# Expert results stored to DRAM and fetched by token, instead of scattered by matmul

## The chip, the cores and the metric

The kernel runs on one core of one Trainium2 chip. The metric is the device time of one execution in microseconds (us), as the median of three runs. A core has TensorE (PE, with PEld its weight loads), VectorE (DVE), ScalarE (ACT), GpSimd (POOL) and SyncE (SP), each with its own queue of instructions; they wait for one another by semaphores. DMA engines move data between DRAM and the core's memories.

## The reference

Four transformer layers over 256 tokens of width 1024, all in f32: two of a first kind, two of a second. The last block of the last layer is a mixture of eight experts, and only this block and what surrounds it are touched:

```python
logits = (xt @ w_router).astype(jnp.float32)
top_vals, top_idx = lax.top_k(logits, TOP_K)          # TOP_K = 2 of 8 experts
probs = jax.nn.softmax(top_vals, axis=-1)
combine = jnp.sum(jax.nn.one_hot(top_idx, N_EXPERTS) * probs[..., None], axis=1)
# for each expert:
acc = acc + c[:, None] * ((silu(xt @ wg) * (xt @ wu)) @ wd)     # wg, wu: 1024 x 2816
# and then
x = layer_norm(DN_ALPHA * x + acc, ln2_g, ln2_b)
```

## The kernel before

Every f32 product is made of three matmuls: an operand is split into a high part (ScalarE's copy, `e_hi`, `ring_hi`) and the rest (VectorE's subtraction, `e_lo`, `ring_lo`); high x high, low x high and high x low are summed in PSUM (`product`, L707 to L709).

An expert handles up to 128 tokens, its slots; were any expert chosen by more than 128 tokens, a second pass over all experts (numbers 8 to 15) would follow under `If(over > 0)`. With the inputs here it is skipped. An expert's weights, 34.6 MB, are cut in 48 units of 704 KB. SyncE loads them into eight buffers (`e_raw`, `expert`, L576) as TensorE frees them (`w_used`); ScalarE makes the high part (L2174), VectorE the low part in place (L3043), TensorE multiplies. Units 0 to 7 and 16 to 23 are the gate's, 8 to 15 and 24 to 31 the up projection's, for one half of the hidden width each; 32 to 47 are the down projection's. Between them VectorE does the gating product (L3049), TensorE transposes it (L1629), ScalarE and VectorE split it (L2183, L3056). Each engine has its order written out by unit number in a loop body (`expert_pe`, `expert_act`, `expert_dve`); expert 0 is unrolled and experts 1 to 7 are a hardware loop (`Fori`).

The tokens of an expert: one-hot tables from ranks (`slots`, L2989) give, by a tiny matmul (`token_of_slot`, L1600), the token of each slot; GpSimd fetches those rows of X from DRAM (`expert_pool`, L3286) and TensorE turns them (`gather`, L1594).

The results: an expert's output stands in the two PSUM banks `Sp` by slot. During the next expert ScalarE evicts its high part (`result`, L2167), VectorE makes its low part (`result_low`, L3028) and one-hot tables slot to token (`slots_to_tokens`, L3032), TensorE multiplies table and result for each half of the tokens (`scatter`, L1606, L1607, behind units 3 and 7), and VectorE adds the sum, times the token's weight for that expert, to the accumulator `ACC` (`add_back`, L2998). After the loop each engine tests for overflow (L1685 on TensorE) and loads the number of experts run; the last expert's result goes the same way in halves (L1694, L1695, L3114), then the norm and the output follow. `ACC` is cleared on VectorE behind the mixer of the last layer (`route_tables`, L2917), and ALPHA x X is added to it behind the last expert (L3105).

Of the kernel before, what the change touches and what calls it, by code (L numbers as in the profile page):

```python
# [134 lines left out]
def build(nc, at, n_const, const_d, w, out_d):  # L135
# [45 lines left out]
    FLAG = sb("FLAG", [P, 2], I32)  # L181
    TOKEN = sb("TOKEN", [P, NTB, 2], F32R)
    ROWS = sb("ROWS", [P, 1], U32)
    rows_d = nc.dram_tensor("rows_of_x", (S, D), F32, kind="Internal").ap()

# [146 lines left out]

    hEh = parts_at("hEh", arena_base, 0, [P, FT2, P])
# [8 lines left out]
    HBe = ar(2 * FT2 * S + HALF, HALF).rearrange("p (j q) -> p j q", j=JT)  # L342
    YBh = parts_at("YBh", arena_base, om + 2560, [P, D])
# [16 lines left out]
    ANY = ar(om + 4608 + 296, NTB * NE).rearrange("p (t e) -> p t e", t=NTB)  # L360
    ROUTE = G[:, 0:NTB, 0:2 * NE].rearrange("p t (w e) -> p t w e", w=2)
# [62 lines left out]
    m_yh, m_y = sig("e_y_high_part"), sig("e_y_taken")  # L424
    m_sc, m_acc = [sig("e_scattered0"), sig("e_scattered1")], sig("tables_cleared_then_e_added")
# [89 lines left out]
    def _(sp):  # L515
# [63 lines left out]
        with sp.Fori(0, NE) as i:  # L579
            expert(i, i)  # L580
        sp.wait_ge(m_flag.sem, 1)
        over = sp.value_load(FLAG[0:1, 0:1], min_val=0, max_val=1)
        with sp.If(over > 0):
            with sp.Fori(NE, 2 * NE) as i:
                expert(i, i - NE)

# [77 lines left out]
    def _(pe):  # L664
# [938 lines left out]
        def scatter(tb):  # L1603
            for h in range(2):
                cs = slice(h * 512, (h + 1) * 512)
                pe.matmul(Sp[:, h, :], PmT[:, tb, :], YBh[:, cs], start=True, stop=False)  # L1606
                last = pe.matmul(Sp[:, h, :], PmT[:, tb, :], YBl[:, cs], start=False, stop=True)  # L1607
            last.then_inc(m_sc[tb].sem, 1)

# [6 lines left out]
        def expert_pe(i, first=False):  # L1616
# [31 lines left out]
            for j in range(4 * KT):  # L1648
# [7 lines left out]
                if j == 3 and not first:  # L1656
                    pe.wait_ge(m_y.sem, i)
                    scatter(0)
                if j == KT - 1 and not first:
                    pe.wait_ge(m_acc.sem, 2 * i + 2)  # L1660
                    scatter(1)
                if first and j == KT:
                    token_of_slot(1)
                if j == KT + 4:
                    if not first:
                        pe.wait_ge(m_acc.sem, 2 * i + 3)
                    pe.wait_ge(m_p.sem, i + 2)
                    token_of_slot(0)
                if j == 2 * KT + 1:
                    hidden_e(0)  # L1670
            pe.wait_ge(m_t.sem, i + 1)
# [5 lines left out]
            gather(i + 1)  # L1677
# [3 lines left out]
        with pe.Fori(1, NE) as i:  # L1681
            expert_pe(i)
        pe.wait_ge(m_flag.sem, 1)
        over = pe.value_load(FLAG[0:1, 0:1], min_val=0, max_val=1)
        with pe.If(over > 0):  # L1685
            with pe.Fori(NE, 2 * NE) as i:
                expert_pe(i)
        n_all = pe.value_load(FLAG[0:1, 1:2], min_val=NE, max_val=2 * NE)
        pe.wait_ge(m_gd.sem, n_all + 1)
# [9 lines left out]
    def _(act):  # L1699
# [464 lines left out]
        def result(n):  # L2164

            act.wait_ge(w_used.sem, n * UNITS_E + U0)
            nc.scalar.activation(YBh[:, :], Sp[:, :, :].rearrange("p b n -> p (b n)"), ACT.Copy).then_inc(m_yh.sem, 1)  # L2167

        def expert_act(i, first=False):
# [15 lines left out]
            for j in range(UNITS_E):  # L2185
                if j == ACT_AHEAD and not first:
                    act.wait_ge(m_p.sem, i + 1)
# [16 lines left out]
                if j == 5 * KT + 2 + ACT_AHEAD:  # L2204
# [4 lines left out]
        with act.Fori(1, NE) as i:  # L2209
            expert_act(i)  # L2210
        act.wait_ge(m_flag.sem, 1)
        over = act.value_load(FLAG[0:1, 0:1], min_val=0, max_val=1)
        with act.If(over > 0):
            with act.Fori(NE, 2 * NE) as i:
                expert_act(i)
        n_all = act.value_load(FLAG[0:1, 1:2], min_val=NE, max_val=2 * NE)
        act.wait_ge(w_used.sem, n_all * UNITS_E + U0)
# [17 lines left out]
    def _(dve):  # L2235
# [455 lines left out]
        for l in range(DEPTH):  # L2691
# [224 lines left out]
            def route_tables():  # L2916
                do(v.memset(ACC, 0.0), m_acc)  # L2917
                do(v.memset(RK, 1e6), m_acc)
                do(v.memset(CW, 0.0), m_acc)
# [75 lines left out]
        def add_back(i, tb):  # L2995
            dve.wait_ge(m_sc[tb].sem, i)
            dve.wait_ge(m_acc.sem, i * 2 + (tb + 1))
# [330 lines left out]
```

## Time and profile before

| | us |
|---|---|
| median of three runs (lowest, highest) | 2000.38 (1999.57, 2001.59) |
| span of the profiled execution, its first to its last instruction | 1997.8 |
| TensorE busy | 1971.7 |
| VectorE busy | 1586.5 |
| ScalarE busy | 1226.4 |
| GpSimd busy | 98.7 |

The page gives no other time of the profiled execution than its span. Engines work side by side, so busy times don't add up; matmuls are pipelined, so their durations overlap and the distance of two starts is what one costs. An idle time is named by what ended it. Times of instructions are from the span's start. The experts' weights are the last 790 us of it.

### The profile page before, as it was taken

What the parts mean: (1) busy time and instruction counts of PE and PEld (TensorE: products, weight loads), DVE (VectorE), ACT (ScalarE), POOL (GpSimd) and SP (SyncE); (2) the same over time, 40 slices, a digit from 0 to 9 for tenths busy, and PEclk for the clock granted to TensorE, in tenths of its full rate; (3) what the DMA queues carried; (4) which work ended last, traced back from release to release, by engine and by line L of the source; (5) the groups of instructions that cost most, each with busy time, mean ns of one, the idle gap of its engine ahead of it and who ended that gap; (6) DMA issues with size and microseconds to landing.
All of it is one profiled execution on the core that took longest, in us unless ns stands there. A gap on an engine that the chain in (4) does not pass through costs nothing.

```text
span 1997.8 us, 30577 instructions
## 1 busy us (share of the span) xinstructions
PE 1971.7 (99%) x11807; PEld 1679.3 (84%) x11807; DVE 1586.5 (79%) x1630; ACT 1226.4 (61%) x1323; POOL 98.7 (5%) x163
## 2 busy tenths in 40 slices
PE   8999999999999999999999999999999999999997
PEld 6888888888888898888889888888888888888886
DVE  7787745868774579776658878999999899999997
ACT  6665534566553457455536537777777777777775
POOL 0400000040000000000000000000000000000000
PEclk9999999999999999999999999999999999999999
DMA  8326555632655555075545209999999999999995
GB/s 302 120 90 212 190 190 179 217 117 95 206 190 190 184 201 168 3 236 190 190 169 196 101 19 388 362 362 366 365 358 368 360 366 365 364 364 363 366 361 199
DMA packets 154089, 481.08 MB, mean 241 GB/s; under 512 B 14608, under 2 KB 41728, under 8 KB 153856
## 3 DMA queue, kind: packets, MB, share of 16 engines
q1 hardware_dynamic: 150064, 465.46, 64.7%
q0 software_dynamic: 3920, 14.16, 2.0%
q8 instruction: 74, 1.21, 0.2%
q14 instruction: 31, 0.25, 0.0%
HBM read 477.48 MB, written 2.10 MB: 240 GB/s over the span
## 4 chain that ended last, share of the span: by engine, by line
PE 91%; DVE 6%; ACT 1%; DMA 1%; issue 1%; POOL 1%; SPq 0%; DVEq 0%; POOLq 0%; ACTq 0%
PE G L707 16%; PE G L709 16%; PE G L708 16%; PE Sp L707 5%; PE Sp L709 5%; PE Sp L708 5%; PE G L1212 3%; PE G L734 3%; PE G L1511 3%; PE G L1213 2%; PE G L694 1%; DVE ring_lo L2251 1%; PE G L1512 1%; PE G L689 1%; PE G L690 1%; PE Sp L1212 1%
## 5 line engine op out<-in xcount | busy, mean ns | idle before, releaser
L2174 ACT ACTIVATE e_hi<-e_raw 128x1408 fp32r<-128x1408 f32 x384 | 523.8, 1381 | 156.4 <-DMA e_raw<-in_moe_w_gate 64.2
L3043 DVE TENSOR_TENSOR e_lo<-e_raw,e_hi 128x1408 fp32r<-128x1408 f32 x384 | 601.9, 1620 | 20.1 <-ACT e_hi L2174 17.6
L2251 DVE TENSOR_TENSOR ring_lo<-ring,ring_hi 128x2048 fp32r<-128x2048 f32 (+2 forms) x171 | 383.5, 2254 | 183.2 <-ACT ring_hi L1714 181.8
L1714 ACT ACTIVATE ring_hi<-ring 128x2048 fp32r<-128x2048 f32 (+1 forms) x179 | 335.5, 1883 | 227.5 <-PE G L709 109.7
L707 PE MATMUL G<-e_hi,xgTh 128*128 128x512 f32 (+1 forms) x768 | 289.2, 377 | 0.1
L709 PE MATMUL G<-e_hi,xgTl 128*128 128x512 f32 (+1 forms) x768 | 288.5, 376 | 0.0
L708 PE MATMUL G<-e_lo,xgTh 128*128 128x512 f32 (+1 forms) x768 | 287.1, 374 | 0.0
L708 PEld LDWEIGHTS G<-e_lo,xgTh 128*128 128x128 f32 x768 | 144.2, 188 | 23.9
L709 PEld LDWEIGHTS G<-e_hi,xgTl 128*128 128x128 f32 x768 | 144.0, 188 | 23.0
L707 PEld LDWEIGHTS G<-e_hi,xgTh 128*128 128x128 f32 x768 | 144.3, 188 | 22.7 <-DVE e_lo L3043 0.4
L707 PE MATMUL G<-ring_hi,xT 128*128 128x512 f32 (+2 forms) x360 | 140.4, 390 | 0.0
L707 PE MATMUL Sp<-e_hi,hEh 128*128 128x512 f32 x352 | 138.4, 393 | 0.0
L709 PE MATMUL G<-ring_hi,xT 128*128 128x512 f32 (+2 forms) x360 | 137.5, 382 | 0.0
L709 PE MATMUL Sp<-e_hi,hEl 128*128 128x512 f32 x352 | 137.4, 390 | 0.0
L708 PE MATMUL G<-ring_lo,xT 128*128 128x512 f32 (+2 forms) x360 | 137.4, 382 | 0.0
L708 PE MATMUL Sp<-e_lo,hEh 128*128 128x512 f32 x352 | 137.2, 390 | 0.0
L1212 PE MATMUL G<-xT,ring_hi 128*128 128x512 f32 x288 | 100.8, 394 | 0.0
L707 PE MATMUL G<-ring_hi,hTh 128*128 128x512 f32 x256 | 100.0, 391 | 0.0
L709 PE MATMUL G<-ring_hi,hTl 128*128 128x512 f32 x256 | 99.7, 389 | 0.0
L708 PE MATMUL G<-ring_lo,hTh 128*128 128x512 f32 x256 | 99.6, 389 | 0.0
L1213 PE MATMUL G<-xT,ring_lo 128*128 128x256 f32 x288 | 79.9, 277 | 0.0
L707 PEld LDWEIGHTS G<-ring_hi,xT 128*128 128x128 f32 x360 | 67.6, 188 | 14.5 <-issue 1.8
(480 smaller groups left out, 3589.9 us busy)
## 6 DMA issues: line engine op xcount, KB each, us to landing
e_raw<-in_moe_w_gate SPq DMA_DIRECT2D x128, 704.0 KB, 6.0
e_raw<-in_moe_w_up SPq DMA_DIRECT2D x128, 704.0 KB, 6.0
e_raw<-in_moe_w_down SPq DMA_DIRECT2D x128, 704.0 KB, 5.9
ring<-in_w_in SPq DMA_DIRECT2D x48, 1024.0 KB, 5.1
ring<-in_w_mlp_up SPq DMA_DIRECT2D x32, 1024.0 KB, 5.2
ring<-in_w_mlp_down SPq DMA_DIRECT2D x32, 1024.0 KB, 4.8
ring<-in_w_out SPq DMA_DIRECT2D x16, 1024.0 KB, 4.8
ring<-in_ffn_w_gate SPq DMA_DIRECT2D x22, 512.0 KB, 3.6
```

Of the source, the lines that this page charges most:

```text
L689: pe.matmul(out, ah, bh, start=start, stop=False, **kw)
L707: pe.matmul(out, ah, bh, start=start, stop=False, **kw)
L708: pe.matmul(out, ah, bl, start=False, stop=False, **kw)
L709: return pe.matmul(out, al, bh, start=False, stop=stop, **kw)
L734: last = pe.transpose(dst, src, ident[0:k, 0:k])
L1212: pe.matmul(out.rearrange("p (w s) -> p w s", w=2), bh[:, k, ms_], xT[:, :, kk, :], start=kk == 0, stop=False, skip_group_check=True)
L1213: last = pe.matmul(out[:, 0:S], bl[:, k, ms_], xTh[:, kk, :], start=False, stop=kk == KT - 1, skip_group_check=True)
L1511: pe.matmul(out.rearrange("p (w s) -> p w s", w=2), bh[:, k, ms_], xT[:, :, kk, :], start=kk == 0, stop=False, skip_group_check=True)
L1714: nc.scalar.activation(ring_hi[:, n % H, 0:m], ring[:, n % R, 0:m], ACT.Copy).then_inc(w_hi.sem, 1)
L2174: nc.scalar.activation(e_hi[:, u, :], e_raw[:, u, :], ACT.Copy).then_inc(w_hi.sem, 1)
L2251: v.tensor_tensor(ring_lo[:, n % R, cs], ring[:, n % R, cs], ring_hi[:, n % H, cs].bitcast(F32), ALU.subtract).then_inc(w_lo.sem, 1)
L3043: v.tensor_tensor(e_lo[:, u, :], e_raw[:, u, :], e_hi[:, u, :].bitcast(F32), ALU.subtract).then_inc(w_lo.sem, 1)
```

## The change

The result of an expert is evicted whole by ScalarE, as f32, into `YB`, and GpSimd stores these 128 rows (512 KB) to a DRAM buffer `y_d` of 16 x 128 rows, one block for each expert run (16 for the second pass). VectorE computes for each token the two rows of `y_d` that hold its results (`rows_of_y`, behind unit 40 of expert 0), and sets `ACC` to ALPHA x X (`scaled_x`, behind units 24 and 28 of expert 0). Both look-ups, for both halves of the tokens, are four fetches by index, which GpSimd issues when the results of experts 0 to 6 are stored; VectorE adds them, times the token's weights, behind units 24, 28, 32 and 36 of the last expert (`y_rows_added`). Therefore the last expert is written out apart, behind the loop (experts 1 to 6) and the test for overflow, on every engine but GpSimd's, with the number of the last run in a register. Its own result still goes by matmul. A token whose row is not yet written (its second expert is the last, or its slot is beyond 128) points to a row of zeros: nine blocks of `y_d`, 7 to 15, are stored as zeros by GpSimd from a cleared buffer of its own, `YZERO`, after the first norm of the third layer. `scatter`, `add_back`, `result_low`, the clearing of `ACC`, the last expert's gather and one `token_of_slot` of expert 0 are gone; `slots_to_tokens` is left for the last result only. Two declarations of semaphores are left out below.

```diff
@@ -178,10 +178,12 @@
-    FLAG = sb("FLAG", [P, 2], I32)
+    FLAG = sb("FLAG", [P, 3], I32)
...
+    YROWS = sb("YROWS", [P, 2 * NTB], U32)
...
+    y_d = nc.dram_tensor("rows_of_y", (2 * NE * P, D), F32, kind="Internal").ap()
@@ -330,6 +332,7 @@
+    YZERO = ar(2 * FT2 * S + 2048, D)
@@ -340,6 +343,7 @@
+    YB = ar(om + 2560, D)
@@ -358,6 +362,11 @@
+    RANKED = ar(om + 4608 + 320, 2 * NTB * NE).rearrange("p (w t e) -> p w t e", w=2, t=NTB)
+    YROW = ar(om + 4608 + 352, 2 * NTB)
+    YLIM = ar(om + 4608 + 356, 2)
+    YSHIFT = ar(om + 4608 + 360, 2 * NTB)
+    YIN = [[XN[:, 0, :], XN[:, 1, :]], [ar(2 * FT2 * S + 2 * HALF + 1024 + tb * D, D) for tb in range(NTB)]]
@@ -576,13 +586,17 @@
-        with sp.Fori(0, NE) as i:
+        with sp.Fori(0, NE - 1) as i:
...
-            with sp.Fori(NE, 2 * NE) as i:
+            with sp.Fori(NE - 1, NE) as i:
+                expert(i, i)
+            with sp.Fori(NE, 2 * NE - 1) as i:
...
+        last = sp.value_load(FLAG[0:1, 2:3], min_val=NE - 1, max_val=2 * NE - 1)
+        expert(last, NE - 1)
@@ -1600,20 +1614,13 @@
-        def scatter(tb):
-            for h in range(2):
-                cs = slice(h * 512, (h + 1) * 512)
-                pe.matmul(Sp[:, h, :], PmT[:, tb, :], YBh[:, cs], start=True, stop=False)
-                last = pe.matmul(Sp[:, h, :], PmT[:, tb, :], YBl[:, cs], start=False, stop=True)
-            last.then_inc(m_sc[tb].sem, 1)
-
...
-        def expert_pe(i, first=False):
+        def expert_pe(i, first=False, final=False):
@@ -1653,40 +1660,36 @@
                 columns_e(j)
-                if j == 3 and not first:
-                    pe.wait_ge(m_y.sem, i)
-                    scatter(0)
-                if j == KT - 1 and not first:
-                    pe.wait_ge(m_acc.sem, 2 * i + 2)
-                    scatter(1)
-                if first and j == KT:
-                    token_of_slot(1)
-                if j == KT + 4:
+                if j == KT + 4 and not final:
...
-                        pe.wait_ge(m_acc.sem, 2 * i + 3)
+                        pe.wait_ge(m_yh.sem, i)
...
-            pe.wait_ge(m_t.sem, i + 1)
+            if final:
+                pe.wait_ge(m_yh.sem, i)
+            else:
+                pe.wait_ge(m_t.sem, i + 1)
...
-            gather(i + 1)
+            if not final:
+                gather(i + 1)
...
-        with pe.Fori(1, NE) as i:
+        with pe.Fori(1, NE - 1) as i:
...
-            with pe.Fori(NE, 2 * NE) as i:
+            with pe.Fori(NE - 1, 2 * NE - 1) as i:
...
-        n_all = pe.value_load(FLAG[0:1, 1:2], min_val=NE, max_val=2 * NE)
-        pe.wait_ge(m_gd.sem, n_all + 1)
+        last = pe.value_load(FLAG[0:1, 2:3], min_val=NE - 1, max_val=2 * NE - 1)
+        expert_pe(last, final=True)
@@ -2164,9 +2167,10 @@
-            nc.scalar.activation(YBh[:, :], Sp[:, :, :].rearrange("p b n -> p (b n)"), ACT.Copy).then_inc(m_yh.sem, 1)
-
-        def expert_act(i, first=False):
+            act.wait_ge(y_stored.sem, n * 16 + 16 * NE)
+            nc.scalar.activation(YB, Sp[:, :, :].rearrange("p b n -> p (b n)"), ACT.Copy).then_inc(m_yh.sem, 1)
+
+        def expert_act(i, first=False, final=False):
@@ -2184,7 +2188,6 @@
-                    act.wait_ge(m_p.sem, i + 1)
@@ -2201,19 +2204,22 @@
-                if j == 5 * KT + 2 + ACT_AHEAD:
+                if j == 5 * KT + 2 + ACT_AHEAD and not final:
...
-        with act.Fori(1, NE) as i:
+        with act.Fori(1, NE - 1) as i:
...
-            with act.Fori(NE, 2 * NE) as i:
+            with act.Fori(NE - 1, 2 * NE - 1) as i:
...
+        last = act.value_load(FLAG[0:1, 2:3], min_val=NE - 1, max_val=2 * NE - 1)
+        expert_act(last, final=True)
+        act.wait_ge(y_stored.sem, n_all * 16 + 16 * NE)
@@ -2914,9 +2920,8 @@
-                do(v.memset(ACC, 0.0), m_acc)
-                do(v.memset(RK, 1e6), m_acc)
-                do(v.memset(CW, 0.0), m_acc)
+                do(v.memset(RK, 1e6))
+                do(v.memset(CW, 0.0))
@@ -2992,11 +2997,24 @@
-        def add_back(i, tb):
-            dve.wait_ge(m_sc[tb].sem, i)
-            dve.wait_ge(m_acc.sem, i * 2 + (tb + 1))
-            v.scalar_tensor_tensor(ACC[:, tb, :], Sp[:, :, :].rearrange("p b n -> p (b n)"), CW[:, tb, bass.ds(i, 1)], ACC[:, tb, :],
-                                   ALU.mult, ALU.add).then_inc(m_acc.sem, 1)
+        def rows_of_y():
+            do(v.tensor_tensor(RANKED, SELECTED, RK[:, :, 0:8].unsqueeze(1).to_broadcast([P, 2, NTB, NE]), ALU.mult))
+            do(v.tensor_reduce(YROW.rearrange("p (w t) -> p w t", w=2), RANKED, AX_X, ALU.add))
+            do(v.tensor_scalar(YLIM[:, 0:1], CNT[:, 3:4], float(P), None, ALU.mult))
+            do(v.tensor_scalar(YSHIFT, YROW, float(P), float((NE - 1) * P), ALU.is_ge, ALU.mult))
+            do(v.tensor_tensor(YROW, YROW, YSHIFT, ALU.add))
+            do(v.scalar_tensor_tensor(YROW.rearrange("p (w t) -> p w t", w=2), IDXF[:, :, 0:2].rearrange("p t w -> p w t"), float(P),
+                                      YROW.rearrange("p (w t) -> p w t", w=2), ALU.mult, ALU.add))
+            do(v.tensor_scalar(YSHIFT, YROW, YLIM[:, 0:1], float(2 * NE * P - 1), ALU.is_ge, ALU.mult))
+            do(v.tensor_tensor(YROWS[:, :], YROW, YSHIFT, ALU.max), y_known)
+
+        def scaled_x(tb):
+            v.tensor_scalar(ACC[:, tb, :], X[:, tb, :], ALPHA, None, ALU.mult).then_inc(y_added.sem, 1)
+
+        def y_rows_added(w, tb):
+            dve.wait_ge(y_in.sem, 16 * 2 * NTB)
+            dve.wait_ge(y_added.sem, NTB * (w + 1))
+            v.scalar_tensor_tensor(ACC[:, tb, :], YIN[w][tb], PR[:, tb, 2 + w:3 + w], ACC[:, tb, :], ALU.mult, ALU.add).then_inc(y_added.sem, 1)
@@ -3005,7 +3023,8 @@
-            do(v.tensor_copy(FLAG[:, :], CNT[:, 1:3]), m_flag)
+            do(v.tensor_scalar(CNT[:, 3:4], CNT[:, 1:2], float(NE), float(NE - 1), ALU.mult, ALU.add))
+            do(v.tensor_copy(FLAG[:, :], CNT[:, 1:4]), m_flag)
@@ -3024,9 +3043,6 @@
-        def result_low():
-            v.tensor_tensor(YBl[:, :], Sp[:, :, :].rearrange("p b n -> p (b n)"), YBh[:, :].bitcast(F32), ALU.subtract).then_inc(m_y.sem, 1)
-
@@ -3036,7 +3052,7 @@
-        def expert_dve(i, first=False):
+        def expert_dve(i, first=False, final=False):
@@ -3056,9 +3072,6 @@
             for j in range(UNITS_E):
-                if j == DVE_AHEAD and not first:
-                    dve.wait_ge(m_yh.sem, i)
-                    result_low()
@@ -3067,18 +3080,20 @@
-                if j == 3 + DVE_AHEAD and not first:
-                    add_back(i, 0)
+                if first and j in (3 * KT, 3 * KT + 4):
+                    scaled_x(int(j > 3 * KT))
+                if first and j == 5 * KT:
+                    rows_of_y()
+                if final and j >= 3 * KT and j % 4 == 0 and j < 5 * KT:
+                    w_, tb = divmod((j - 3 * KT) // 4, NTB)
+                    y_rows_added(w_, tb)
...
-                    if first:
-                        dve.wait_ge(m_i.sem, 1)
-                        do(v.tensor_tensor(SLOTS[:, 0:2], Sp[:, 1, 0:1].to_broadcast([P, 2]), c("less"), ALU.add))
+                    if final:
+                        slots_to_tokens()
...
-                        add_back(i, 1)
-                    slots_to_tokens()
-                    slots(i + 1)
-                if j == 2 * KT + DVE_AHEAD - 1:
-                    dve.wait_ge(m_i.sem, i + 2)
+                        slots(i + 1)
+                if j == 2 * KT + DVE_AHEAD - 1 and not final:
+                    dve.wait_ge(m_i.sem, i + 1)
@@ -3088,21 +3103,20 @@
-                if j == 5 * KT + 2 + DVE_AHEAD:
+                if j == 5 * KT + 2 + DVE_AHEAD and not final:
...
-        with dve.Fori(1, NE) as i:
+        with dve.Fori(1, NE - 1) as i:
...
-            with dve.Fori(NE, 2 * NE) as i:
+            with dve.Fori(NE - 1, 2 * NE - 1) as i:
...
-        dve.wait_ge(m_acc.sem, n_all * 2 + 1)
-        for tb in range(NTB):
-            do(v.scalar_tensor_tensor(ACC[:, tb, :], X[:, tb, :], ALPHA, ACC[:, tb, :], ALU.mult, ALU.add))
+        last = dve.value_load(FLAG[0:1, 2:3], min_val=NE - 1, max_val=2 * NE - 1)
+        expert_dve(last, final=True)
@@ -3111,6 +3125,7 @@
             dve.wait_ge(z_s.sem, 2 * h + tb + 1)
+            dve.wait_ge(y_added.sem, NTB * 3)
@@ -3277,6 +3292,10 @@
+                step(pool, g.memset(YZERO, 0.0), pstep)
+                for i in range(NE - 1, 2 * NE):
+                    pool.dma_start(y_d[i * P:(i + 1) * P, :], YZERO).then_inc(y_stored.sem, 16)
+                pool.wait_ge(y_stored.sem, 16 * (NE + 1))
@@ -3285,14 +3304,24 @@
+            pool.wait_ge(m_yh.sem, i + 1)
+            pool.dma_start(y_d[i * P:(i + 1) * P, :], YB).then_inc(y_stored.sem, 16)
+
...
-        for i in range(NE):
+        for i in range(NE - 1):
...
-            for i in range(NE, 2 * NE):
+            for i in range(NE - 1, 2 * NE - 1):
...
+            pool.wait_ge(y_stored.sem, 16 * 3 * NE)
+        pool.wait_ge(y_stored.sem, 16 * 2 * NE)
+        pool.wait_ge(y_known.sem, 1)
+        for w_ in range(2):
+            for tb in range(NTB):
+                q = w_ * NTB + tb
+                g.indirect_dma_start(YIN[w_][tb], None, y_d, bass.IndirectOffsetOnAxis(YROWS[:, q:q + 1], 0)).then_inc(y_in.sem, 16)
```

## Rows read from the trace of the kernel before

**Rows 1.** The page, part 1: busy time, share and instructions of TensorE

```profile
PE 1971.7 (99%) x11807; PEld 1679.3 (84%) x11807; DVE 1586.5 (79%) x1630; ACT 1226.4 (61%) x1323; POOL 98.7 (5%) x163
```

**Rows 2.** Stretches: length, busy of PE, PEld, DVE, ACT, POOL, clock, DMA share, GB/s

```profile
870.00:880.00 10.00, 10.00 (x46) 8.29 (x45) 6.82 (x6) 5.36 (x4) 0.00 (x0) 1.00 0.64 215
1222.00:1226.00 4.00, 4.00 (x21) 3.43 (x20) 4.00 (x3) 3.34 (x3) 0.00 (x0) 1.00 1.01 420
1402.60:1499.20 96.60, 96.60 (x462) 82.47 (x461) 89.01 (x63) 71.51 (x54) 0.94 (x1) 1.00 0.97 362
```

**Rows 3.** Waits from 1190 us on: who for whom, total us, times, longest

```profile
PEld G L1629 <- DVE ARENA L3049: 1.1, 1, 1.1
...
SPq L576 <- PE G L709: 392.5, 256, 12.2
```

**Rows 4.** TensorE in order of time: start, us, instruction, count

```profile
1295.84 1.03 PE L1594 MATMUL G<-C,AT_ 128*128 128x128 f32 x8
1296.62 0.48 PE L707 MATMUL Sp<-e_hi,hEh 128*128 128x512 f32 x1
...
1507.23 0.40 PE L1606 MATMUL Sp<-YBh,PmT 128*128 128x512 f32 x1
...
1508.16 0.39 PE L707 MATMUL G<-e_hi,xgTh 128*128 128x512 f32 x1
...
1913.02 0.28 PE L1600 MATMUL Sp<-TOKEN,Pm 128*128 128x2 f32 x2
1913.16 0.48 PE L707 MATMUL G<-e_hi,xgTh 128*128 128x512 f32 x1
...
1982.76 0.39 PE L709 MATMUL Sp<-e_hi,hEl 128*128 128x512 f32 x1
```

**Rows 5.** VectorE by line, one expert: count, busy us, mean ns, idle before

```profile
L2998 DVE SCALAR_TENSOR_TENSOR ARENA<-Sp,ARENA 128x1024 f32<-128x1024 f32 x2 | 2.6, 1284 | 1.2 <-PE Sp L1607 1.1
L3028 DVE TENSOR_TENSOR YBl<-Sp,YBh 128x1024 fp32r<-128x1024 f32 x1 | 1.2, 1225 | 1.1 <-ACT YBh L2167 1.1
```

**Rows 6.** VectorE in order of time, behind its last low part

```profile
1978.88 2.48 DVE L3105 SCALAR_TENSOR_TENSOR ARENA<-X,ARENA 128x1024 f32<-128x1024 f32 x2
```

**Rows 7.** TensorE's sequencer at the test: ns least/median/most, first and last start

```profile
L1685 PEldq COMPARE_BRANCH  x1: 3529/3529/3529, 1980.2 to 1980.2; - x1
...
L1689 PEldq ALU_OP  x1: 36/36/36, 1984.5 to 1984.5; - x1
```

**Rows 8.** DMA queues from 1981 to 1982 us: packets, MB, share

```profile
q8 instruction: 1, 0.02, 6.8%
```

**Rows 9.** VectorE in order of time, units 21 to 40 of expert 4

```profile
1637.16 10.83 DVE L3043 TENSOR_TENSOR e_lo<-e_raw,e_hi 128x1408 fp32r<-128x1408 f32 x7
...
1661.12 2.75 DVE L3049 TENSOR_TENSOR ARENA<-ARENA,G 128x1408 f32<-128x1408 f32 x1 [0.91 <-PE G L709]
...
1669.82 4.70 DVE L3043 TENSOR_TENSOR e_lo<-e_raw,e_hi 128x1408 fp32r<-128x1408 f32 x3
```

**Rows 10.** TensorE in the same stretch: the transposes, unit 38's first use

```profile
1664.97 1.36 PE L1629 MATMUL G<-C,ARENA 128*128 128x128 f32 x11
...
1673.00 0.39 PE L707 MATMUL Sp<-e_hi,hEh 128*128 128x512 f32 x1
```

**Rows 11.** VectorE in order of time: the accumulator's clearing

```profile
1189.72 1.76 DVE L2917 MEMSET ARENA<- 128x2048 f32 x1 [0.49 <-DVE X L2673]
```

**Rows 12.** DMA issues, whole span, then 1629.2 to 1633.2: KB, us to landing

```profile
e_raw<-in_moe_w_gate SPq DMA_DIRECT2D x128, 704.0 KB, 6.0
...
e_raw<-in_moe_w_gate SPq DMA_DIRECT2D x1, 704.0 KB, 7.8
AT_<-rows_of_x,ROWS POOLq DMA_INDIRECT x1, 8.4
```

**Rows 13.** The two stores of X's rows (L3274)

```profile
DMA to landing us min/median/max: 8.4/10.2/12.0
```

**Rows 14.** GpSimd in order of time, at the dense FFN's norm

```profile
1035.76 1.57 POOL L3146 TENSOR_TENSOR SM<-SM,C 128x1 f32<-128x1 f32 x1 [168.40 <-DVE SM L2649]
```

More of the change, by code:

```diff
@@ L423, in build @@
     m_p, m_g, m_gd, m_ga = sig("e_slots"), sig("e_gathered"), sig("e_gather_taken_dve"), sig("e_gather_taken_act")
-    m_yh, m_y = sig("e_y_high_part"), sig("e_y_taken")
-    m_sc, m_acc = [sig("e_scattered0"), sig("e_scattered1")], sig("tables_cleared_then_e_added")
+    m_yh = sig("e_y_evicted")
+    y_stored, y_known, y_in = sig("e_y_stored"), sig("rows_of_y_known"), sig("rows_of_y_landed")
+    y_added = sig("rows_of_y_added")
     f_sum, f_mean, f_sq = sig("final_sum"), sig("final_mean"), sig("final_squares")
```

## Prediction, before the change was run

> **What bounds the kernel now.** I read the page first (how full is each engine), then the busy time by stretch of single experts, the waits of the expert stage, and the order of the instructions on TensorE and VectorE there. TensorE is busy for 1971.7 of 1997.8 us [rows 1]. The expert stage fills the last 790 us: one expert of the loop takes 96.6 us, TensorE is busy for all of them, VectorE for 89.0, ScalarE for 71.5, and the DMA engines move 362 GB/s with a busy share of 0.97 [rows 2]. A full DMA looks like a second bound; the waits say otherwise. In the whole stage TensorE's largest wait for another engine is 1.1 us (for the gated hidden units, in the first expert), while SyncE, which issues the weight loads, waits 392.5 us for TensorE to free a buffer [rows 3]. So transfers follow TensorE's pace, and a matmul taken out of the loop shortens it, until loads or VectorE's low parts come too late.
>
> **What TensorE loses.** In the order of its instructions a scatter is four 512-column matmuls: it starts at 1507.23 and the next weight matmul starts at 1508.16, 0.93 us [rows 4]. There are two scatters in each of experts 1 to 7, one for each half of the tokens: 14 x 0.93 = 13.0 us. The last expert also loses its gather, a row fetch for an expert that doesn't exist: 0.78 us from 1295.84 to 1296.62 for the eight transposes, and about 0.1 us in the slower start of the next matmul. One look-up of tokens by slot goes in the last expert and one in expert 0: 1913.02 to 1913.16 and 0.1 us behind, 0.24 us each, 0.5 us [rows 4]. Removed: 13.0 + 0.9 + 0.5 = 14.4 us. The waits for the add-backs that go with it cost nothing now. VectorE loses 1.2 (low part) + 2 x 1.28 us (add-backs) [rows 5] and two small tables per expert, so its load falls from 89.0 of 96.6 to at most 85.2 of 94.7 us: in a loop expert VectorE is not what is late next. The tail behind the last weight matmul (eviction, low part, eight matmuls, sums, norm) stays; the two sums with X, 2.48 us, leave it, but VectorE did them under TensorE's last matmuls [rows 6], so that gives nothing.
>
> **The branch moves into the middle.** The test for overflow stood behind the last expert, where TensorE waited for the last result anyway. It now stands between expert 6 and expert 7. Before, TensorE's sequencer reached the branch at 1980.2 and spent 3529 ns in it; the register load and its arithmetic behind it end with the sum for the next wait at 1984.5 [rows 7]. The last matmul started at 1982.76 [rows 4] and another could have followed 0.23 us later. In the middle of the stage TensorE therefore stands from one point to the other plus about 0.15 us: 1984.55 - 1982.99 + 0.15 = 1.7 us, once. Lower end 0 (the sequencer gets further ahead); upper end 4.8 us, the 3.5 us of the branch on top of the later steps with none of it ahead. One packet of the instruction queue runs during this branch [rows 8]. The Trainium skill (Runtime: NRT & Kernel Launch, Instruction fetch mechanics) says that a taken branch whose target is outside the fetched pages waits for a DMA of the target's page. By that rule, the trace agrees: the stall is a fetch and stays, wherever the branch is put; were it only the end of a full queue, the cost would be about the same 1.7 us. On VectorE the same branch and loads end before its running instruction does: its sums with X start at 1978.88, as its last low part ends [rows 6]. I count 0 for it, ScalarE and SyncE, with up to 1.5 us for one of them in the range.
>
> **VectorE's new work.** Lead is the time from the end of a unit's low part to TensorE's first use of it. In a loop expert seven low parts in a row, units 21 to 27, take 10.83 us, one of them 1.62, so they follow each other every 1.535 us [rows 9]. Units 21 to 34 would need 14 x 1.535 = 21.5 us; the gating product behind them starts 23.96 us after unit 21's part did, so VectorE was idle for 2.5 us of it. In the last expert four sums of 1.2 us (a sum of the same size, two in 2.48 [rows 6]) fall behind units 24, 28, 32 and 36. Three of them, 3.6 us, lie before the product: it is 1.1 us late and done near 1665.0 instead of 1663.9. TensorE begins to transpose it at 1664.97 [rows 10]: 0.1 us lost. The fourth sum comes before the low part of unit 38, back to back from there on, which ended at 1671.4 [rows 9]: now 1671.4 + 1.1 + 1.2 = 1673.7, where TensorE wants it at 1673.0 + 0.1 [rows 10]. Another 0.6 us and some 0.1 for each wake-up, together 0.9 us; 0 if the lead won in the branch's stall lasts, 4.8 if none of the four sums is covered. Expert 0 gets two scalings of X and eight small table steps, at most 2.5 + 1.7 us, in two places where the same idle time and a lead of 2 us cover them: 0.1 us, up to 1.5. One more table step stands before the second half of the first tokens, where TensorE has no lead: 0.2 us. The accumulator's memset goes, 1.76 us at 1189.72 on VectorE [rows 11]; TensorE was in weight matmuls until 1194.5 and the chain after that starts from its last product, so 0, at best -0.3.
>
> **The transfers.** A loop expert gets a store of 0.5 MB beside its 34.6 MB of weights and the 0.5 MB row fetch: 35.7 MB in 94.7 us, 377 GB/s. With eight loads queued the engines moved 420 GB/s over 4 us [rows 2]. A buffer is freed seven units before its next content is used, 7 x 94.7/48 = 13.8 us; the load lands 6.0 us after its issue [rows 12], the conversions on ScalarE and VectorE take some 3. So 4 us or more of delay is covered; a row fetch that ran beside the loads made one land after 7.8 us [rows 12], 1.8 later, and TensorE did not wait. The store is as large: 0 us each, and nobody reads it for 95 us. On the POOL queue the store stands behind the row fetch and waits for the eviction; the next fetch is wanted some 30 us later. In the last expert the store (up to 12.0 us to landing, as X's rows [rows 13]) and four fetches (issue 0.94 us each [rows 2], landing 8.4 [rows 12], and up to 5 us for 2.1 MB at 420) end some 31 us into the expert; VectorE asks for them behind unit 24, some 46 us in. Their 2.6 MB take 6.2 us of the engines at 420 GB/s against about 4 us of cover and 1.5 us made good meanwhile: 0.5 us lost, 0 to 3. The nine stores of zeros (4.7 MB) and a memset start near 873 us, under the dense FFN, where POOL waits 168.4 us [rows 14]; the ring's loads take 215 GB/s then [rows 2], half of the 420: 0, up to 2 us if they go ahead of the ring's.
>
> **Sum.** -14.4 + 1.7 + 0.9 + 0.1 + 0.2 + 0.5 = -11.0 us. Span 1997.8 - 11.0 = 1986.8. The page gives the profiled execution only as its span; the median of the timed runs, 2000.38, lies 2.6 us above it, taken as unchanged: 1989.4 us.
>
> **Rivals.**
> A, transfers become the bound and the kernel slower. If the sustained rate is the steady experts' 362 GB/s, not the 420 of 4 us, 0.52 MB more is 1.45 us per expert, and TensorE's saving is lost as well. Experts 1 to 6: +8.7 us; the last gets 2.1 MB more (store and four fetches, less its own fetch): +5.8; the branch is absorbed. 2000.4 + 14 = 2014 us. It decides from a rate below about 370 GB/s. For it: a busy share of 0.97 and ScalarE starting as a load lands. Against: SyncE waits for TensorE, and 420. The Trainium skill (DMA: Bandwidth & Descriptors, Where 436 GB/s comes from) gives a limit of about 358 GB/s per core for HBM traffic; by it an expert would take 99.6 us, an estimate from that page. The trace disagrees: 362 over whole experts already, 420 at the peak. 9%.
> B, the gain is partly eaten: the branch at its upper end, or a fetch miss on a second engine, and the last expert's sums and fetches at their ends: -14.4 + 4.8 + 4 + 3 = -2.6, 1997.8 us; with half of that 1994. 12% for 1994 to 1999.
> C, the scatter was hidden anyway, since units wait for low parts: 2000.4 + 3 of new stalls, no change within 0.2% or a bit above. Against: TensorE's matmuls follow each other at 0.23 us across the scatter. 4%.
> D, nothing new costs: -14.4 - 0.3, 1985.7 us. 8%.
>
> **How the numbers follow.** The forecast's own case, 1986 to 1994, has 67%. The range leaves out A and the far end of B: 1985.5 to 1996.0. A timing of this kernel can tell 0.2%, 4 us, from no change. Faster by more than that (below 1996.4): the forecast, D and nearly all of B, 0.84; within: 0.06; slower: A and the worse part of C, 0.10.
>
> **What would show it.** Loop experts of 94.7 us (A: over 97); one gap of about 1.7 us on TensorE before expert 7, with the branch's 3.5 us; waits of TensorE for the gating product and one low part in the last expert, 1 us together; loads landing up to 8 us after issue while a store runs, and TensorE waiting for none; the dense FFN unchanged. Wrong would be a TensorE that waits for low parts in loop experts.

## The result: 2008.5 us, slower by 0.4%

| | median of the runs, us | least to most | ratio to before, 95% interval | profiled span |
|---|---|---|---|---|
| before | 2000.1 | 1999.6 to 2001.6 | | 1997.8 |
| after | 2008.5 | 2007.3 to 2009.8 | 1.0043 [1.0031, 1.0055] | 2006.8 |

The forecast was 1989.4 us, faster, in a range of 1985.5 to 1996.0. The kernel got slower, and its time lies outside that range.

By the page's busy times alone the kernel after looks lighter than the one before. The line, TensorE first:

```profile
PE 1967.5 (98%) x11739; PEld 1673.3 (83%) x11739; DVE 1562.2 (78%) x1601; ACT 1224.4 (61%) x1322; POOL 114.4 (6%) x183
```

Against [rows 1], TensorE has 68 matmuls fewer and is busy 4.2 us less, in a span that is 9.0 us longer. So 13 us are idle time that before didn't have, and some of the busy time ran at a lower clock. Where the loss lies is seen when the start of each weight matmul is set against the start of the same matmul of before. The offset, after less before, in us of the profiled executions:

| part | offset at its end | change | forecast |
|---|---|---|---|
| up to expert 1 (zero stores, expert 0) | +12.4 | +12.4 | +0.1 |
| experts 1 to 6 | +1.8 | -10.6 | -11.2 |
| branch, until the clock is back | +8.8 | +7.0 | +1.7 |
| rest of expert 7 | +8.6 | -0.2 | -1.5 |
| tail | +9.0 | +0.4 | 0 |

Of the first 12.4, 0.7 are there before the first zero store is issued (874 us), where both kernels run the same code; in the profiles of the other runs this early offset is between -0.2 and 2.2 us. The stage with the zero stores adds 12.3, and 0.6 are won back between it and expert 1. So an offset between two profiles says nothing finer than about 2 us, but what it gains or loses within a stage does.

**The loop experts** do what was forecast: 94.90 us each from one first matmul to the next, 96.65 before. Expert 3 by stretch (length, busy of PE, PEld, DVE, ACT, POOL, granted clock, DMA share, GB/s), beside the third row of [rows 2]:

```profile
1508.40:1603.30 94.90, 94.90 (x454) 81.06 (x453) 85.55 (x58) 71.99 (x55) 1.53 (x2) 1.00 0.98 377
```

377 GB/s, as worked out, and no wait of TensorE: rival A's sustained limit of 362 GB/s isn't there.

**The zero stores** cost the most. The ring is the set of buffers into which SyncE loads the weights of the dense layers, as `e_raw` is for the experts. The same columns for the dense FFN (the first row answers to the first of [rows 2]), and behind them a stretch further on, of after and then of before:

```profile
870.00:880.00 10.00, 10.00 (x46) 8.28 (x45) 7.54 (x6) 3.80 (x3) 5.70 (x10) 1.00 0.68 222
880.00:890.00 10.00, 9.41 (x51) 7.79 (x49) 2.29 (x1) 1.92 (x1) 0.00 (x0) 1.00 1.04 413
890.00:900.00 10.00, 1.84 (x7) 1.75 (x8) 4.75 (x4) 5.37 (x6) 0.00 (x0) 0.57 1.07 385
900.00:910.00 10.00, 10.00 (x54) 8.59 (x54) 6.64 (x6) 5.23 (x5) 0.00 (x0) 0.92 0.38 118
...
910.00:984.00 74.00, 74.00 (x421) 64.16 (x420) 46.30 (x40) 38.74 (x39) 0.00 (x0) 1.00 0.59 188
```

```profile
910.00:984.00 74.00, 74.00 (x428) 65.20 (x427) 47.22 (x41) 39.26 (x41) 0.00 (x0) 1.00 0.56 186
```

Read the DMA columns first: full for 20 us, then 118 GB/s, because the ring's buffers are full again and SyncE waits 11.2 us, until 906.06, for TensorE to free one. The 40 us moved 11.4 MB. Both streams together ask for 13.4 MB in that time, an estimate from 217 GB/s over the same 40 us of before and 4.7 MB of zeros; at the 413 GB/s seen here 40 us have room for 16.5. So the rate was enough over 40 us, but not while the burst lasted. ScalarE and VectorE show what failed: one conversion each between 880 and 890. In order of time, with the idle time before each instruction and what ended it:

```profile
885.51 1.92 ACT L1717 ACTIVATE ring_hi<-ring 128x2048 fp32r<-128x2048 f32 x1 [7.34 <-DMA ring<-in_ffn_w_up]
...
887.53 2.29 DVE L2257 TENSOR_TENSOR ring_lo<-ring,ring_hi 128x2048 fp32r<-128x2048 f32 x1 [8.35 <-ACT ring_hi L1717]
...
893.27 1.91 ACT L1717 ACTIVATE ring_hi<-ring 128x2048 fp32r<-128x2048 f32 x1 [5.85 <-DMA ring<-in_ffn_w_up]
895.22 2.29 DVE L2257 TENSOR_TENSOR ring_lo<-ring,ring_hi 128x2048 fp32r<-128x2048 f32 x1 [5.39 <-ACT ring_hi L1717]
897.42 0.68 DVE L2948 TENSOR_TENSOR ARENA<-ARENA,G 128x512 f32<-128x512 f32 x1
898.16 1.11 PE L748 MATMUL G<-C,ARENA 128*128 128x128 f32 x4 [8.74 <-DVE ARENA L2948]
```

TensorE's wait bears the name of a product on VectorE (897.42). That product stands in VectorE's queue behind a low part (895.22), which waited for a high part (893.27), which waited for a load. The loads of the ring from 870 to 905 us, as their line's view gives them, after and then before:

```profile
L570 SPq DMA_DIRECT2D ring<-in_ffn_w_gate x5: 367/1276/2447, 874.3 to 892.3; - x5
L570 SPq DMA_DIRECT2D ring<-in_ffn_w_up x5: 510/1701/5532, 874.7 to 893.6; - x5
...
DMA to landing us min/median/max: 4.7/9.7/15.8
```

```profile
L560 SPq DMA_DIRECT2D ring<-in_ffn_w_gate x7: 367/368/368, 873.6 to 900.3; - x7
L560 SPq DMA_DIRECT2D ring<-in_ffn_w_up x7: 508/508/509, 874.0 to 900.7; - x7
...
DMA to landing us min/median/max: 3.4/4.0/4.8
```

The latest load lands 11 us later than in before (15.8 for 4.8), and SyncE needs up to 5.5 us to issue one (0.5 before). 9.0 us pass from one matmul to the next, 1.6 more are lost at the lower clock, and 1.7 creep in until some 1000 us (seven matmuls fewer in the 74 us shown).

**The branch.** The sequencer's view of the test, and the stretches behind it:

```profile
L1688 PEldq COMPARE_BRANCH  x1: 5842/5842/5842, 1885.3 to 1885.3; - x1
```

```profile
1888.00:1892.00 4.00, 0.24 (x2) 0.00 (x0) 3.85 (x3) 3.36 (x3) 0.02 (x1) 0.93 1.01 417
1892.00:1896.00 4.00, 3.90 (x10) 3.33 (x11) 2.92 (x3) 3.37 (x3) 0.53 (x1) 0.50 1.02 406
1896.00:1900.00 4.00, 4.00 (x14) 3.23 (x14) 2.47 (x3) 2.15 (x2) 0.79 (x1) 0.71 0.69 233
```

5842 ns, where [rows 7] had 3529; 4.25 us from matmul to matmul, and then 7 us in which the granted clock is 0.50 to 0.71: 10 matmuls in 4 us instead of 20. That is the 1.2 GHz level at first. By the offsets the pause costs 4.0 us and the clock behind it 2.9, together 7.0 us. In before the DMA engines stood idle during the branch, as the same columns of before show:

```profile
1980.00:1984.00 4.00, 3.14 (x14) 2.25 (x12) 1.45 (x3) 0.82 (x2) 0.00 (x0) 1.00 0.02 4
```

**SyncE's own test for overflow**, which stands between the loads of expert 6 and those of expert 7, stalls as well. The branch and the next instruction of its sequencer, then its issues around them (start, length, count), and the DMA engines meanwhile:

```profile
L593 SPq COMPARE_BRANCH  x1: 50/50/50, 1873.9 to 1873.9; - x1
...
L598 SPq TENSOR_LOAD <-FLAG x1: 284/284/284, 1878.9 to 1878.9; - x1
...
1869.15 3.73 SPq L586 DMA_DIRECT2D e_raw<-in_moe_w_down  x3
1879.57 3.59 SPq L586 DMA_DIRECT2D e_raw<-in_moe_w_gate  x5
...
1878.00:1881.00 3.00, 3.00 (x18) 2.60 (x17) 1.74 (x3) 2.86 (x3) 0.00 (x0) 1.00 0.28 37
```

The branch's record is short, but nothing follows it for 5 us. SyncE issues no weight load for 6.7 us, and the DMA engines run dry, at 37 GB/s. This is in every run with the changed order of the experts, 4.6 to 5.4 us each time, whether or not TensorE has a branch. Why SyncE stalls was not tested. On VectorE and ScalarE the next instruction of the sequencer comes 0.6 and 0.5 us after the branch.

**The last expert** has the two waits that were forecast, one of them larger. From the waits of 1190 us on (who for whom, total us, times, longest), beside the first of [rows 3]:

```profile
PEld G L721 <- issue: 4.3, 1, 4.3
...
PEld G L1636 <- DVE ARENA L3065: 2.7, 3, 1.7
```

and how long the weight loads took to land, of after from 1892 to 1925 us and of before from 1888 to 1935:

```profile
DMA to landing us min/median/max: 3.8/8.9/10.3
```

```profile
DMA to landing us min/median/max: 5.6/6.0/8.0
```

The gating product costs 1.4 us (1.67 us between two matmuls instead of 0.23), unit 38 0.7 us.

### The profile page after: what moved, and what is told of

It reads as the page before. It is cut to its first block, busy times and chain, and to the rows that moved or that the text cites. A ratio compares the mean times of both kernels' runs of the same rounds, so it can differ in the third digit from the quotient of the medians.

```text
span 2006.8 us, 30329 instructions
## 1 busy us (share of the span) xinstructions
PE 1967.5 (98%) x11739; PEld 1673.3 (83%) x11739; DVE 1562.2 (78%) x1601; ACT 1224.4 (61%) x1322; POOL 114.4 (6%) x183
## 4 chain that ended last, share of the span: by engine, by line
PE 85%; DVE 8%; DMA 3%; issue 2%; ACT 1%; POOL 1%; SPq 0%; DVEq 0%; POOLq 0%; ACTq 0%
PE G L721 15%; PE G L723 15%; PE G L722 15%; PE Sp L721 5%; PE Sp L723 5%; PE Sp L722 5%; PE G L1226 3%; PE G L748 3%; PE G L1525 3%; DVE e_lo L3059 2%; DVE ring_lo L2257 2%; PE G L1227 1%; PE G L708 1%; PE G L1526 1%; PE G L703 1%
## 5 line engine op out<-in xcount | busy, mean ns | idle before, releaser
L1226 PE MATMUL G<-xT,ring_hi 128*128 128x512 f32 x288 | 100.8, 393 | 0.0
L1525 PE MATMUL G<-xT,ring_hi 128*128 128x512 f32 x224 | 80.9, 404 | 0.0
```

The costliest lines, as they stand in the source:

```text
L1226: pe.matmul(out.rearrange("p (w s) -> p w s", w=2), bh[:, k, ms_], xT[:, :, kk, :], start=kk == 0, stop=False, skip_group_check=True)
L1525: pe.matmul(out.rearrange("p (w s) -> p w s", w=2), bh[:, k, ms_], xT[:, :, kk, :], start=kk == 0, stop=False, skip_group_check=True)
```

## Experiments

Theories to begin with: Z, the nine stores cost 12 us by delaying the ring's loads; K, the branch costs 7 us; L, in the last expert store and fetches delay the weight loads, and the branch's pause hides part of that. The rivals stand with each run. None of the runs takes out SyncE's stall, which is a rival of L: it too makes the last expert's loads late.

**One zero store** (`z1_one_block`). Eight of the nine stores are left out; the blocks of a second pass share the place of the first eight.

```
-    for i in range(NE - 1, 2 * NE):
+    for i in range(NE - 1, NE):
         pool.dma_start(y_d[i * P:(i + 1) * P, :], YZERO)
```

> The changed kernel with one block of zeros stored (0.5 MB) instead of nine (4.7 MB); rows_of_y has eight blocks, so a second pass, which these inputs do not take, would write over the first. Theory Z (the nine stores starve the ring's loads in the dense FFN: TensorE stands 9 us there and runs at the lower clock after it, 12.4 us lost by the first expert): 2008.5 - 12.4 = 1996, loads of the ring at 873 to 885 land within 6 us again. Rival (the expert stage's own transfers cost it; the zeros only shift it): 2006 to 2009. Rival (one queued memset and wait on GpSimd is what delays the third layer): 2008.

1996.5 us, ratio 0.998 [0.9971, 0.999]; 12.0 below after. No gap near 889 us, and the offset doesn't grow in that stage (1.5 us before it and behind it).

**The stores alone, in the kernel before** (`z2_before_plus_zeros`).

```
+    step(pool, g.memset(YZERO, 0.0), pstep)
+    for i in range(NE - 1, 2 * NE):
+        pool.dma_start(y_d[i * P:(i + 1) * P, :], YZERO).then_inc(y_stored.sem, 16)
+    pool.wait_ge(y_stored.sem, 16 * (NE + 1))
     layer_norm()
```

> The kernel before with only the memset, the nine stores of zeros and the wait for them added after the first norm of the third layer. Theory Z: 2000.1 + 12.4 = 2012.5, with one gap of TensorE of 9 us near 889 us and a lower clock right behind. Rival (nothing to do with the zeros): 2000.

2012.1 us, 1.0059 [1.0042, 1.0075]: 11.8 us above before. The wait is there without the rest of the change:

```profile
PEld G L737 <- DVE ARENA L2946: 9.0, 1, 9.0
```

**No branch on TensorE**, with the nine stores (`b1_no_branch_pe`) and with one (`c1_both`). The bound of the loop is read before it, so a second pass is more turns of the same loop.

```
-    with pe.Fori(1, NE - 1) as i: ...
-    over = pe.value_load(...)
-    with pe.If(over > 0): ...
     last = pe.value_load(...)
+    with pe.Fori(1, last) as i:
+        expert_pe(i)
```

> The changed kernel, on TensorE alone without the test for overflow: its loop over experts runs from 1 to the number of the last run, loaded from FLAG ahead of the loop, and the last expert's code follows the loop directly. Zeros as in the changed kernel. Theory B (the taken branch waits for a fetch of code, 5.8 us in the sequencer under full DMA load, 4.0 us of idle TensorE and 2.8 us of lower clock): the gap before expert 7 goes, -6.8 us. Theory L (the gap also gave VectorE a lead of 7 to 8 us, which the four fetches then ate): 3 to 4 us of it come back as waits for low parts in units 10 to 18 of the last expert, so 2005. Rival (the gap is the drain of TensorE's queue at any loop end): no change, 2008.

> Both edits: one block of zeros (a second pass, not taken here, would write over the first) and no test for overflow on TensorE. If the two losses are independent: the sum of both, 2008.5 - 12.4 - 3.3 = 1993, and without theory L 1989. If each only uncovers the other, not below 1996.

2005.4 us, 1.0023 [1.0013, 1.0032], and 1993.2 us, 0.9965 [0.9953, 0.9976]: each 3.1 to 3.3 below its fellow with the branch, not 7. TensorE's pause before expert 7 is gone; new waits appear in that expert. Waits of `c1_both` from 1880 to 1935 us:

```profile
PEld G L721 <- DVE e_lo L3055: 3.5, 4, 1.1
...
PEld G L1636 <- DVE ARENA L3061: 2.1, 1, 2.1
```

So K holds, and some 3.7 of the 7.0 us are given back in the last expert. The waits are where L puts them, but L isn't the only cause that fits. In `c1_both` SyncE's stall stands too: the load of expert 7's first unit is issued 8.5 us before TensorE uses it (13.5 us in expert 5), and the low parts of the first four units are ready 0.9 to 1.3 us ahead instead of 2.5 to 3.6. Store and fetches then meet a lead that is already half gone; by unit 12 it is 0.06 us. In after TensorE's pause covered this, with 12.5 us from issue to use. What each of the two causes costs isn't separated by these runs.

**Stores one at a time** (`z3_spaced`) and **by threes** (`z4_threes`), nothing left out.

```
     for i in range(NE - 1, 2 * NE):
         pool.dma_start(y_d[i * P:(i + 1) * P, :], YZERO).then_inc(y_stored.sem, 16)
-    pool.wait_ge(y_stored.sem, 16 * (NE + 1))
+        pool.wait_ge(y_stored.sem, 16 * (i - NE + 2))        # z4_threes: at every third only
```

> The changed kernel with its nine zero stores one at a time: each is issued once the one before has landed; nothing is left out. Theory B (burst): the stall before 898 us comes from nine stores in flight at once beside the ring's loads; one at a time they take 0.5 MB each, the ring's loads keep their place, TensorE's 9.0 us gap and the slow clock behind it go: as with one store, 1996 us. Rival V (volume): the 4.7 MB must be moved anyway and the dense stage has no room for them: about 2008 us, with the same 9 us of waits, in smaller pieces.

> The changed kernel with its nine zero stores in three groups of three, each group issued once the one before has landed; nothing is left out. Landing times of the ring's loads so far: at most 15.8 us with nine stores in flight (gap 9.0 us), 9.8 us with one at a time (gap 1.4 us). Theory T (the gap is the landing time above what the ring's slots cover, and that grows with the number of stores in flight): three in flight give at most 11 to 13 us, a gap of 3 to 5 us, about 2000 us. Rival N (any burst, however short, costs the whole gap; or none below nine): 2008 or 1997 us.

1997.0 us, 0.9985 [0.9976, 0.9995], and 2002.1 us, 1.0006 [0.9997, 1.0016]. The ring's landing times (least, median, most), one at a time over 870 to 925 us, and by threes over 870 to 905:

```profile
DMA to landing us min/median/max: 3.8/5.9/9.8
```

```profile
DMA to landing us min/median/max: 4.7/8.2/11.9
```

and what TensorE waited in `z4_threes`, 870 to 910 us:

```profile
PEld G L748 <- DVE ARENA L2948: 1.7, 1, 1.7
...
PEld G L1525 <- DVE ring_lo L2257: 1.2, 1, 1.2
```

Same bytes, and 1, 3 or 9 in flight give at most 9.8, 11.9 and 15.8 us to landing and 1997, 2002 and 2008.5 us. The volume (V) isn't the cost: one at a time, 4.7 MB cost 0.5 us by the times, 1.0 by the ratios and 1.3 within the stage by the traces more than 0.5 MB. By threes the stage loses 4.4 us, in small waits (2.9 us) and again in the slower pace behind them (421 matmuls from 910 to 984 us).

**Smaller pieces** (`p1_zeros_1kb`, `p2_zeros_1kb_rows`), all nine at once again; in the second the ninth block is stored whole. ZEROS stands for `YZERO[:, 0:256].unsqueeze(1).to_broadcast([P, 4, 256])`.

```
-    pool.dma_start(y_d[i * P:(i + 1) * P, :], YZERO)
+    pool.dma_start(y_d[i * P:(i + 1) * P, :].rearrange("p (c n) -> p c n", c=4), ZEROS)      # p1
+    dst = y_d[b * P:(b + 4) * P, c4 * 256:(c4 + 1) * 256].rearrange("(b p) n -> p b n", b=4)
+    pool.dma_start(dst, ZEROS)                                                               # p2: b in 7, 11; c4 in 0 to 3
```

> The changed kernel with the nine zero stores still issued at once, but each row cut into four pieces of 1 KB, so that their packets are as large as those of the ring's loads. Theory P (the queues take turns packet by packet, so 4 KB packets take four times the ring's share): the ring now gets about half of 420 GB/s, 210, above the 185 that it takes in this stage; TensorE's gap shrinks from 9.0 to under 3 us: 1996 to 1999 us. Rival Q (the share goes by bytes or by the transfers waiting in the queues, whatever the packet): gap 8 to 10 us, 2008 us.

> The changed kernel; eight of its nine zero stores write 256 columns of four blocks instead of 1024 columns of one, so that each piece of DRAM is 1 KB and can't be joined to the next (cutting the rows alone had left 1584 packets of 3.6 KB). Same 4.7 MB, still all issued at once. Theory P (the queues take turns packet by packet): about 5000 packets of 1 KB, the ring gets half of the rate, above what it takes in this stage; the gap at 889 us falls from 9.0 to under 3 us: 1996 to 1999 us. Rival Q (the share goes by the transfers waiting, whatever the packet): gap 8 to 10 us, about 2008 us.

2010.6 us, 1.0053 [1.0036, 1.007], and 2008.8 us, 1.0041 [1.0026, 1.0057], gaps of 10.1 and 9.7 us. But neither made the packets smaller; the queues of `p2_zeros_1kb_rows` from 868 to 905 us:

```profile
q1 hardware_dynamic: 5280, 5.24, 40.6%
q0 software_dynamic: 1572, 5.72, 39.5%
```

5.72 MB in 1572 packets is 3.6 KB each, as in after. So Q's time came out, but P wasn't tested by it: the size of the packets, on which P rests, didn't change, and whether the queues share by packets stays open.

**A short body behind the branch** (`t1_short_body`, one zero store). Test, branch and register loads stay. The run has a second edit, which its expectation leaves out: GpSimd issues each of the last expert's fetches only when the one before has landed.

```
     with pe.If(over > 0):
-        with pe.Fori(NE - 1, 2 * NE - 1) as i:
-            expert_pe(i)
+        pe.wait_ge(m_flag.sem, 1)
...
         q = w_ * NTB + tb
+        if q:
+            pool.wait_ge(y_in.sem, 16 * q)
         g.indirect_dma_start(YIN[w_][tb], None, y_d, ...)
```

> The kernel with one zero store and TensorE's branch (1996.5 us), with the body that TensorE jumps over cut to one wait (the case of more than 128 tokens in an expert is left out on TensorE). Theory F (the price of the branch is the fetch of code that lies behind the long body): the branch instruction's 5.8 us and TensorE's gap of 5.0 us before expert 7 fall to under 2.5 us; the time between 1993 and 1995 us, since the last expert's loads give part back. Rival R (any jump and its register load cost this beside full queues, whatever is jumped): gap 5.0 us, 1996.5 us.

1990.8 us, 0.9951 [0.9934, 0.9968], 5.8 below `z1_one_block` by the ratios, for both edits together. The branch, and the waits for low parts from 1880 to 1935 us:

```profile
L1688 PEldq COMPARE_BRANCH  x1: 213/213/213, 1872.7 to 1872.7; - x1
...
PEld G L721 <- DVE e_lo L3058: 1.2, 2, 0.9
```

213 ns for 5842 (6577 in `z1_one_block`), and no gap. Neither branch nor register loads are the price, but that the next code lies behind a body of a whole expert: F. The Trainium skill (Runtime: NRT & Kernel Launch, Instruction fetch mechanics) says that a taken branch to a page not yet fetched waits for it; by that rule, the trace agrees. The other engines fit F too, though no run varies their bodies: VectorE and ScalarE, which jumped in 0.6 and 0.5 us, have 114 and 117 records in a loop expert's trace, TensorE has 452 matmuls and their weight loads, and SyncE, which stalled for 5 us, has 174 and jumps over two such bodies. The time came out below the expected 1993 to 1995. The second edit fits that: TensorE waits 1.2 us for low parts against 3.5 in `c1_both`, and the latest weight load lands after 11.1 us against 13.3. The next run, which has the fetches apart too, shows the same (0.8 and 10.6 us).

**Fetches apart** (`f3_fetches_paced`, on `c1_both`).

```
+    if final and j in (10, 16, 22):        # ScalarE, behind high_part(j)
+        nc.scalar.activation(YSHIFT[:, j // 6:j // 6 + 1], YLIM[:, 0:1], ACT.Copy).then_inc(y_turn.sem, 1)
...
-    dve.wait_ge(y_in.sem, 16 * 2 * NTB)      # VectorE, in y_rows_added(w, tb)
+    dve.wait_ge(y_in.sem, 16 * (w * NTB + tb + 1))
...
         q = w_ * NTB + tb
+        if q:
+            pool.wait_ge(y_turn.sem, q)
+            pool.wait_ge(y_in.sem, 16 * q)
         g.indirect_dma_start(YIN[w_][tb], None, y_d, ...)
```

> The kernel with one zero store and without TensorE's branch (1993.2 us), with the last expert's four fetches apart: fetch 1, 2 and 3 wait until ScalarE has passed units 10, 16 and 22 and until the fetch before has landed; VectorE's sums wait for their own fetch. Theory L (fetches and store at once delay the ring's loads): TensorE's gaps of 1.05, 1.10, 1.00 and part of the 2.17 us between 1900 and 1915 go, 3 to 4 us: about 1989.5 us. Rival W (the waits come from VectorE, which is full in that expert): they stay, 1993 us.

1991.4 us, 0.9954 [0.9937, 0.9971]; 1.8 below `c1_both` by the medians, and in the profiled spans 1.3 (1989.0 for 1990.3), of which 1.1 in the last expert. Waits from 1880 to 1935 us:

```profile
PEld G L1637 <- DVE ARENA L3064: 2.5, 1, 2.5
...
PEld G L722 <- DVE e_lo L3058: 0.8, 3, 0.4
```

The waits for low parts fall from 3.5 to 0.8, as L says; that for the gating product grows from 2.1 to 2.5. So the fetches account for 1 to 2 us of the 3.7 that were given back, if the gain is real: the intervals of the two runs overlap. The lead still falls to 0.06 us at unit 12, and SyncE's stall (5.0 us here) is untouched.

**All together, nothing left out** (`best_full`): stores one at a time, no branch on TensorE, fetches apart.

> Nothing is left out: the changed kernel with its nine zero stores one at a time, TensorE's experts 1 to the last but one in one loop whose bound is read before it (no branch), and the last expert's fetches apart. From the runs before: 1997.0 (stores one at a time) less 3.3 (branch and the give-back beside it, from 1996.5 against 1993.2) less 1.8 (fetches apart) = 1992 us by the theory that the three add up; 1994 or more if the zero stores' last ones or the fetches' waits come back elsewhere.

1992.4 us, 0.9957 [0.9943, 0.997]: 8 us faster than before, 16 than after. The three parts add up. SyncE still stalls 5.4 us at its branch.

## Why the prediction was wrong

- **The zero stores, "0, up to 2 us if they go ahead of the ring's": wrong, and the step that turned the sign.** It measured 12.0 and 11.8 us in two kernels. The argument compared rates, 215 GB/s taken of 420, and they do fit: one at a time costs about 1 us. What wasn't asked was how late a single load may land. With nine stores in flight one landed after 15.8 us. The kernel before had a sign of how thin the cover was: ScalarE waited three times for the ring's loads there, 2.5 us from 870 to 905 us, with landings of at most 4.8 us. The prediction had made this very test for the experts (13.8 us of cover against landing and conversions) and left it out for the stage with the biggest burst.
- **The branch, 1.7 us with an upper end of 4.8: right mechanism, wrong size.** 7.0 in the trace; taking it out alone gave 3.1 and 3.3 us by runs, since the last expert gave the rest back. Its own duration was taken over from a place where the DMA engines had little left to do; beside a full stream of weights it took 2.3 us longer, and that made the pause 4.0 us instead of 1.7. And the pause cost a second time, 2.9 us, by the lower clock behind it, which no term of the sum held. That the stall is a fetch fits `t1_short_body`; read as advice it would have said not to jump over the long body.
- **"I count 0" for the same branch on VectorE, ScalarE and SyncE: right for the first two, wrong for SyncE.** SyncE stalled for 4.9 us (4.6 to 5.4 over the runs), above the 1.5 allowed for one of them, in the middle of the weight loads. What that costs in time no run isolates.
- **Scatters, -13.0: right.** 1.75 us per loop expert for 1.86. Loop experts of 94.90 us were forecast as 94.7, at 377 GB/s.
- **The last expert: too optimistic.** Less its scatters, look-up and gather (3.0) plus 1.5 of waits should be -1.5. It is -0.2, and without the branch's pause, in `t1_short_body`, +1.6 (offset -10.9 at its start, -9.3 at its end). "0.1 us" for the gating product is 1.4 to 2.3; for unit 38 0.7, within the 0.9. With "0.5 us, 0 to 3" for the fetches, the error was to count on the 4 us of cover that a loop expert has: weight loads landed up to 10.3 us after issue beside them (8.0 before), SyncE's stall had taken part of that cover, and only TensorE's pause gave VectorE a lead of 8.3 us at unit 3, of which 0.06 were left at unit 14.
- **Rivals.** A gave the sign, not the mechanism: the steady rate was enough, in a burst it wasn't. B's 4.8 us for the branch is near the pause itself (4.0), without the clock behind it; its "fetch miss on a second engine" happened, on SyncE. C and D fell.

## What to carry over

A transfer added under a stage with half the bandwidth free is hidden only if the stream's loads may land later by the time that the whole burst takes (here 4.7 MB, and loads up to 11 us late). Compare the landing time with the cover of the buffers, not GB/s with GB/s, and issue a bulk of stores one after the other. A jump over a long body cost TensorE 4 us and the clock behind it, and SyncE 5 us without loads; look for it on every engine that has the test. More turns of the same loop, with a bound read early, did the same work without it on TensorE; on SyncE this wasn't tried. Time won on the bound engine is given back where another engine's lead was thin: redo the lead for the new pace.

## What the runs showed that was not expected

- The same branch took 3529 ns with idle DMA engines (4 GB/s), 5842 ns beside 417 GB/s, and 213 ns with a short body. Over all runs it is 3.5 and 3.9 us at the end of the kernel and 5.8 to 6.6 in the six kernels that jump over the long body ahead of the last expert. That the load of the DMA engines makes the difference is argued, not tested: place and load changed together.
- The granted clock stood at 0.50 for 6.8 us behind TensorE's pause of 4.2 us (1891.5 to 1898.3 us), 2.9 us lost. In the pause of 9.0 us it fell while TensorE still waited (891.4 to 901.6 us), so only 3.4 us of it met matmuls, 1.6 us lost. In `z3_spaced` and `p1_zeros_1kb` pauses of 4.2 and 4.4 us were followed by 3.4 us at 0.50 only.
- With nine 512 KB stores queued from GpSimd, SyncE's own issue of a load took up to 5.5 us instead of 0.5.
- Behind the stall of the zero stores TensorE ran 1.6% slower at a granted clock of 1.00 until some 1000 us (421 for 428 matmuls from 910 to 984), in most kernels with the stall and in the one by threes, but not in `p1_zeros_1kb` (429), which issued the same nine stores. Its cause stays open, as does the rule by which the two queues share the engines.
